# A hybrid attention step: VectorE takes the low parts ahead of the maxima, ScalarE fewer exponentials ahead of the rounding copy

## The reference

```python
s = jnp.einsum('bqhd,bshd->bhqs', qb, k).astype(jnp.float32) * scale
s = s + cq[..., None] - ct[:, :, None, :]          # forgetting attention: a bias per key
s = jnp.where(kpos[None, :] <= qpos[:, None], s, -jnp.inf)
p = jax.nn.softmax(s, axis=-1).astype(v.dtype)
return jnp.einsum('bhqs,bshd->bqhd', p, v)
```

## Time and profile before

| what | us |
|---|---|
| median of 3 runs | 1362.47 |
| lowest and highest of them | 1362.08, 1365.36 |
| the profiled execution, its own time | 1361.38 |
| its span, from the first to the last instruction | 1359.6 |
| stretch 298 to 420, forgetting attention: VectorE busy | 104.38 |
| stretch 432 to 553, sparse attention: VectorE busy | 104.74 |

### The profile page before, as it was taken

One profiled execution on the slowest core, in us unless ns is written; L12 is line 12 of the kernel. 1 busy time (PEld: TensorE's weight loads), 2 busy tenths in 40 slices (PEclk: granted clock), 3 DMA queues, 4 the chain that ended last, 5 costly groups with the idle time before them and its releaser, 6 DMA issues.

```text
span 1359.6 us, 23602 instructions
## 1 busy us (share of the span) xinstructions
PE 1319.8 (97%) x8868; PEld 1180.4 (87%) x8868; DVE 956.6 (70%) x1795; ACT 676.8 (50%) x1250; POOL 542.7 (40%) x518
## 2 busy tenths in 40 slices
PE   7989999999999999999999999999999999999997
PEld 7859999987877777777899999999999997778886
DVE  4399989898886989768855645555645556576497
ACT  5579979838885888610343223233223233343330
POOL 3406684542322122335645555455565452000011
PEclk9999999999999999999999999999999999999999
DMA  7102432269684622612045434445344359777452
GB/s 247 56 16 67 154 110 78 62 156 217 171 216 99 151 49 43 206 51 70 17 140 179 135 130 155 133 163 179 132 133 155 131 193 349 265 279 251 170 185 110
DMA packets 150369, 197.17 MB, mean 145 GB/s; under 512 B 28120, under 2 KB 106872, under 8 KB 150256
## 3 DMA queue, kind: packets, MB, share of 16 engines
q1 hardware_dynamic: 150256, 195.67, 46.8%
HBM read 136.69 MB, written 48.38 MB: 136 GB/s over the span
## 4 chain that ended last, share of the span: by engine, by line
PE 54%; DVE 3%; DMA 1%; issue 0%; ACT 0%; POOLq 0%; POOL 0%; DVEq 0%; SPq 0%; ACTq 0%
PE banks L2889 32%; PE banks L2261 6%; PE banks L2987 5%; PE banks L2989 5%; PE banks L2988 5%; PE banks L3005 1%; DMA down_raw<-in_w_down 1%; PE banks L2863 0%; DVE rows L3375 0%; DVE h_B_lo L3278 0%; DVE h_T_lo L3278 0%; PE banks L2359 0%; PE banks L2357 0%; ACT h_T_hi L3061 0%; DVE sample_T L3290 0%
## 5 line engine op out<-in xcount | busy, mean ns | idle before, releaser
L3163 POOL TENSOR_TENSOR w_lo<-w_S,w_hi 128x512 fp32r<-128x512 f32 x88 | 119.2, 1354 | 109.9 <-ACT w_hi L3042 109.9
L2889 PE MATMUL banks<-h_T_hi,w_hi 128*128 128x264 f32 x704 | 144.6, 285 | 0.2 <-DVE h_T_lo L3278 0.2
L2889 PE MATMUL banks<-h_T_lo,w_hi 128*128 128x264 f32 x704 | 143.7, 285 | 0.0
L2889 PE MATMUL banks<-h_T_hi,w_lo 128*128 128x264 f32 x704 | 142.9, 283 | 0.0
L3141 ACT CAST down_hi<-down_raw 128x1024 fp32r<-128x1024 f32 x77 | 80.7, 1051 | 121.4 <-PE banks L2989 62.8
L3042 ACT CAST w_hi<-w_S 128x512 fp32r<-128x512 f32 x88 | 54.7, 622 | 167.3 <-PE banks L2889 147.4
L2233 POOL TENSOR_TENSOR ln_rstd<-ln_var_eps,ln_power 128x1 f32<-128x1 f32 (+1 forms) x18 | 25.1, 1393 | 254.5 <-DVE ln_var_eps L2224 136.7
L3243 DVE TENSOR_TENSOR down_lo<-down_raw,down_hi 128x1024 fp32r<-128x1024 f32 x77 | 93.7, 1237 | 43.7 <-ACT down_hi L3141 43.5
L2987 PE MATMUL banks<-down_hi 128*128 128x512 f32 x308 | 120.9, 392 | 0.7 <-DVE down_lo L3243 0.4
L2989 PE MATMUL banks<-down_hi,down_lo 128*128 128x512 f32 x308 | 120.5, 391 | 0.0
L2988 PE MATMUL banks<-down_lo,down_hi 128*128 128x512 f32 x308 | 120.4, 391 | 0.0
(11 more groups left out here) (424 smaller groups left out, 3784.4 us busy)
## 6 DMA issues: line engine op xcount, KB each, us to landing
down_raw<-down_a SPq DMA_DIRECT2D x77, 256.0 KB, 4.1
gate_raw<-in_w_gate SPq DMA_DIRECT2D x11, 1024.0 KB, 6.5
down_t<-in_w_down SPq DMA_DIRECT2D x44, 256.0 KB, 4.0
down_w<-down_t SPq DMA_DIRECT2D x22, 512.0 KB, 3.4
down_raw<-in_w_down SPq DMA_DIRECT2D x22, 512.0 KB, 6.5
down_raw<-down_w SPq DMA_DIRECT2D x44, 256.0 KB, 4.3
up_raw<-in_w_up SPq DMA_DIRECT2D x10, 1024.0 KB, 6.3
down_a<-down_s SPq DMA_DIRECT2D x10, 1024.0 KB, 4.1
```

The lines of the kernel that those rows point to most:

```text
L2889: mm = nc.tensor.matmul(pp[:, bank[to] + ch, 0:PIECE], l, x[name][:, k, ch * PIECE:(ch + 1) * PIECE], start=opens and k == 0 and i == 0, s ...
L3163: nc.gpsimd.tensor_tensor(w_lo[n % 2][:, :, :], weight(m, SCHEME[q][0]), f32(w_hi[n % 2][:, :, :]), ALU.subtract).then_inc(w_lo_done, 1)
```

## The change

In every slot of both attentions VectorE takes the low part of the slot's step (with the reciprocals, if the step opens a batch) ahead of the maxima of the slot's items, and no longer behind them. `plan` numbers them so. ScalarE, in a slot that opens a batch, takes ahead of the rounding copy only the waiting exponentials up to the last one that belongs to the opening batch; the rest comes behind the copy. In the last slots, which have no step, it still takes all.

```diff
@@ plan
         for batch in slot.joined:
             did += 1
             batch.joined = did
+        if slot.step and not slot.step.sample:
+            did += 1
+            slot.step.split = did
         for it in slot.logits:
             did += 1
             it.biased = did
-        if slot.step and not slot.step.sample:
-            did += 1
-            slot.step.split = did
@@ attention, ScalarE
         for slot in slots:
-            if slot.step is None or slot.step.firsts():
-                for it in waiting:
-                    exp(it)
-                waiting = []
+            firsts = slot.step.firsts() if slot.step else [it.batch for it in waiting]
+            soon = max([i + 1 for i, it in enumerate(waiting) if it.batch in firsts], default=0)
+            for it in waiting[:soon]:
+                exp(it)
+            waiting = waiting[soon:]
@@ attention, VectorE
             if dve_beside:
                 dve_beside(dve, slot, 0)
-            for it in slot.logits:
-                biased_max(it)
             x = slot.step
             if x and not x.sample:
                 for batch in x.firsts():
@@
                 nc.vector.tensor_tensor(eT_lo[s][:, x.cols], pt[:, x.k % TR_BANKS, x.cols], f32(eT_hi[s][:, x.cols]),
                                         ALU.subtract).then_inc(freed, 1)
+            for it in slot.logits:
+                biased_max(it)
             if dve_beside:
                 dve_beside(dve, slot, 1)
```

## The result

The changed kernel takes 1389.03 us (median of 4 runs, 1388.73 to 1389.85), the kernel before, run beside it on the same chip, 1362.28 (4 runs, 1361.6 to 1365.36). The ratio is 1.0195, with an interval of 1.0183 to 1.0207: slower by 26.7 us. The direction and the mechanism were forecast, the size was not: 1379.5 was forecast, and 1389.0 lies outside the 1373 to 1385 that had most of the chance, near the upper end of the wide range (1366 to 1391).

The account below looks back on a forecast made before the run. The attentions were taken as bound by handing on between engines, none full. Forgetting +7 and sparse +10 gave 17 us on 1361.38, 1378.4; the runs' median lies 1.1 above, so 1379.5; 8-in-10 range 1366 to 1391.

Parts of the forecast that it names:

- the next pair: Forgetting attention: deferred exponential ahead of the copies of slots 7 and 8 starts the new slot 0's low part 0.3 later; +1.1.
- the ends of the forgetting attention: Forgetting attention's first and last pairs: first among seven given +1.0 each, last, with only small items, given nothing; sum +7.
- the upper bound of what was given: Forgetting attention: +1.0 us for each of 7 pairs, with bounds 0.8 and 1.1.
- The walked pair: First sparse pair, followed slot by slot: later maxima delay slot 6's transposes and slot 8's opening; together +1.7 us.
- two links: First sparse pair: slot 6's transposes +1.1, then slot 8's opening another 0.61, behind slot 7's low part.
- the three short pairs: Sparse attention: three of the first seven pairs, counted with the first link alone, 1.1 each, 3.3 us together.
- the long ones: Sparse attention: four of the first seven pairs, counted at 1.7 each, 6.8 us together.
- The bound of 6.0 us on its gain: Both attentions: ScalarE's edit gains at most TensorE's waits for low parts, 3.6 + 2.4 = 6.0 us.
- the 3.6 of the rows: Forgetting attention: TensorE's 7 waits for low parts, 3.6 us; ScalarE's edit takes away about 0.5 a pair.
- The dearer rival: Both attentions: delays feed on each other, slots with items of 640 keys or more pay 0.61; about 1390 us, chance 0.10.
- The three cheaper rivals: Both attentions: faster, 1356.5 (chance 0.08); no change, 1362.5 (0.06); half, only the forgetting attention pays, about 1369 (0.13).
- the prediction's estimate: Both attentions: by the drain rule a low part holds the maximum 1.1 us, not 0.61; sum 14 x 0.5 = 7 us higher.

Follow-up runs that it names:

- the far one: ScalarE's new order, and VectorE's low part first only in slots none of whose items frees an area the very next slot wants, against the kernel before: 1376.09 us.
- the two last ones: Kernel before with ScalarE's new block in the forgetting attention only, then in the last sparse pair as well: 1361.03 and 1360.87 us.
- the late one: Kernel before with VectorE taking each low part one slot later, behind the next slot's maxima, ScalarE's block old: 1378.22 us, ratio 1.0115.

## Why the prediction came out as it did

**The order on VectorE** was read rightly. The low part is first and waits, and the maximum behind it is what TensorE wants. Step by step, counted from slot 0's transposes: slot 2's copy forecast at 5.24 us, measured 5.54; its low part 5.84 and 6.15; the maximum 6.45 and 6.75; slot 3's transposes 7.33 and 7.63, against 6.16 before. The 0.3 is what the text gave for "the next pair", and it is in each of the middle ones. Its other half, from slot 3 to the next slot 0, was forecast at 7.9 and is 7.94. The three pairs forecast at 46.3 us took 46.71 (15.57 each):

```profile
sum 46.71, PE 42.42 PEld 34.75 DVE 37.94 ACT 36.02 POOL 15.00; mean PE 14.14 PEld 11.58 DVE 12.65 ACT 12.01 POOL 5.00
```

**The first mis-sized term is the ends of the forgetting attention**: +10.5 for +7. The six pairs in the middle grew by 6.6 us, 1.1 each, the upper bound of what was given. But the last pair was given nothing, because its items are small, and grew by 2.0; and the first, given 1.0, grew by 1.9. In the last pair TensorE waits for maxima in slots 1 and 2 (1.26 and 0.84 us) where it waited once, for 0.62. A small item makes the maximum shorter, but not the wait for the copy ahead of it.

**The second is the sparse attention**: +17.2 for +10. The walked pair had two links, 1.1 and 0.6. TensorE in that pair after, for the earlier trace rows:

```profile
451.82 0.66 PE L1449 MATMUL banks<-ident,dsa_exp_a 128*128 128x128 f32 x4 [0.28 <-DVE dsa_nmax L1623]
...
457.99 0.66 PE L1449 MATMUL banks<-ident,dsa_exp_a 128*128 128x128 f32 x4 [1.07 <-DVE dsa_nmax L1623]
...
463.42 0.66 PE L1449 MATMUL banks<-ident,dsa_exp_c 128*128 128x128 f32 x4 [0.51 <-ACT dsa_exp_c L1528]
```

Slot 0's transposes start at 449.16, so slot 6 comes 8.83 us after them (457.99), 7.34 before: +1.5 for +1.1. The missing 0.4 is a link ahead of the two, at slot 2, whose transposes now wait 0.28 for the maximum of slot 1. To slot 8 it is 14.26 us against 12.07, +2.2 for +1.7. What the count did with it is worse: the three short pairs were given one link because they are short, 3.3 us in all, and grew by 7.0; the long ones were given 6.8 and grew by 9.7, of which 1.0 is the clock's; the last got 0 and grew by 0.6. The pair of 6 slots, given 1.1 and grown by 2.9, shows what the count missed:

```profile
501.78 0.66 PE L1449 MATMUL banks<-ident,dsa_exp_b 128*128 128x128 f32 x4 [0.91 <-DVE dsa_nmax L1623]
...
504.05 0.65 PE L1449 MATMUL banks<-ident,dsa_exp_b 128*128 128x128 f32 x4 [0.23 <-DVE dsa_nmax L1623]
...
507.05 0.66 PE L1449 MATMUL banks<-ident,dsa_exp_b 128*128 128x128 f32 x4 [0.87 <-DVE dsa_nmax L1623]
```

Three of its six transposes wait for a maximum, where one did before (0.41). The row of 1.12 above, the opening of the next batch, adds the 1.0 of ScalarE's edit. But length doesn't tell how many links a pair has: the pairs of 8 and 6 slots grew by 3.1 and 2.9, that of 7 by only 0.9, those of 9 and 11 by 3.3 and 1.4. Each would have had to be walked.

**The ScalarE edit** was said to cost nothing beyond what was counted, since its exponentials are wanted late. In the forgetting attention that holds. It is wrong where a lower batch has so few steps that the upper one opens in the next slot: 1.12 us in the row above, 1.0 for that pair by the two kernels that differ in it alone. The bound of 6.0 us on its gain was right for the old order (nothing measurable came of it). Its share for the forgetting attention, the 3.6 of the rows, was too low for the new order, which makes more of the waits that it removes: 5.5 us.

**The rest.** Low parts' waits at slot 0 are gone and everything behind the attentions has its old length, as written. Busy times were to stay within 1 us: VectorE's and ScalarE's grew by 1.5 and 1.3, TensorE's, whose ends are modelled, by 3.4. The clock was to stay, since waits of up to 1.4 us stood in stretches at 1.00; the term was put at nothing and is about 1.0 us. The granted clock is 1.00 in the stretch of the forgetting attention and 0.99 in that of the sparse one, and the longest wait of a weight load there is 2.3 us. VectorE's idle time ahead of low parts was to be "12 or more" in the forgetting attention; it is 25.2. The waits for maxima grew by 15.8 and 15.4 us, where 7 and 10 were written.

**The dearer rival** (1390) has the right number, but not the right mechanism. It let delays feed on each other, priced by the 0.61 of the low part in every slot with a large item. The middle pairs of the forgetting attention don't show it: they repeat at 15.57 us, each with the same delay. What was added is more links, small items among them, and not growing ones. The three cheaper rivals fell by one number, VectorE's 50.2 us ahead of low parts: it was not late enough for the copies, and the sparse attention, which was to buffer it with items two slots apart, lost more than the other. The rule of the Trainium skill that VectorE drains behind each instruction (VectorE: DVE Perf Modes, "The DRAIN you can't avoid") would by the prediction's estimate have given some 24 us, closer to the result, yet for a reason that the rows exclude: the maximum starts at 339.78, 0.60 after the low part's start and 0.09 before its end. The prediction left out that the same section lets an instruction that isn't held start earlier, with which these rows agree. The time lost is ahead of the low part, not behind it.

**What stays open.** That some 40% of the loss is queueing on ScalarE and 60% the longer chain comes from kernels whose exponentials are short but not gone, so that everything else moves too; it is a size, not a proof for each slot. Why the first pair of the forgetting attention pays nearly twice what the others pay was only read, from two waits of 1.32 and 1.73 us in it (0.49 and 0.44 before), and not tried. Why the wait for `key_bias` comes and goes between kernels, and what lets the clock fall, is not explained either.

## What to carry to other kernels

On an engine that works in order, an instruction whose input is not yet there must not stand ahead of one whose input is, above all when the second is wanted sooner: here that order alone cost 33 us of 1362, with VectorE at 86% of the stretch. The reverse, a slot later, cost 16 us, so when a hand-written order is suspected, walk one period with the durations of the trace, for each engine, and count every slot that hands something on, small and short ones too. And a deferral is free only up to the first consumer: look for the shortest case (here a batch with one step), not the usual one.

## What was unexpected of the hardware

With over a quarter of ScalarE's busy time taken out of both attentions, the kernel before gained only 7.7 us of 1362 (ratio 0.9951, 0.9934 to 0.9967): at 79 and 86% busy it was not the bound, and the granted clock stayed at 1.00. The cost of a link is in the work, not in passing it on: VectorE starts 0.04 us after ScalarE's copy ends (338.57 + 0.57 = 339.14, low part at 339.18).

Between 295 and 590 us of the profiles TensorE's granted clock fell to its lower level in six of the kernels, and not in the kernel before: in the same sparse pair of the changed kernel, of the one with the sparse attention alone and of the far one (from 539.95, 534.46 and 528.79), between the attentions in the two last ones, and behind them in the late one (from 571.21). Where the same matmuls stand at both levels it cost 1.0 us (the sixth sparse pair) and 1.6 (twelve matmuls, 4.61 against 3.06), as much as several of the effects weighed here. Before a small difference between two profiles is explained by waits, the granted clock of the stretch should be compared.
